# Mean products one row further back, and one weight half behind the last convolution

## The reference

```
x = layernorm(alpha * x + mixer(x))
x = layernorm(alpha * x + convffn(x))
```

```
gate, rnn = split(x @ w_in_c)
xc = causal_conv4(rnn)
r, i = sigmoid(xc . w_gate_a + b), sigmoid(xc . w_gate_x + b)   # 8 blocks of 128
log_a = 8 * r * log_sigmoid(lambda);  a = exp(log_a)
h = scan(a, sqrt(1 - a^2) * i * xc)
m = (gelu(gate) * h) @ w_out_c
```

## Time and profile before

| | |
|---|---|
| median of 3 runs | 1429.51 us |
| profiled execution | 1428.99 us |
| its span | 1426.9 us |
| TensorE busy | 1404.5 us (98%) |
| VectorE busy | 836.3 us (59%) |
| ScalarE busy | 620.4 us (43%) |
| GpSimd busy | 96.7 us (7%) |
| granted TensorE clock, mean | 0.997 |

### The profile page before, as it was taken

How to read it: one execution, slowest core, us unless ns; L and a number is a source line. 1 busy time by engine, 2 the same in 40 slices (tenths; PEclk the granted TensorE clock), 3 DMA queues, 4 the chain that set the end, 5 groups by cost and what they waited for, 6 DMA issues and landing times.

```text
span 1426.9 us, 24580 instructions
## 1 busy us (share of the span) xinstructions
PE 1404.5 (98%) x10244; PEld 1379.0 (97%) x10244; DVE 836.3 (59%) x1274; ACT 620.4 (43%) x1018; POOL 96.7 (7%) x112
## 2 busy tenths in 40 slices
PE   7999999999999999999999999999999999999996
PEld 7999999999999999999999999999999999999996
DVE  6656665656855644534455778888645455344555
ACT  5443535444654143412343577646632334124334
POOL 0010100000400000000000310024100000000002
PEclk9999999999999999999999999999999999999998
DMA  8131222234222322222222211222223222222222
GB/s 282 51 122 60 80 87 76 92 101 151 72 89 62 102 74 90 74 89 74 80 84 79 83 62 60 89 60 89 74 75 96 83 85 79 89 74 90 83 81 82
DMA packets 37231, 125.18 MB, mean 88 GB/s; under 512 B 4352, under 2 KB 6528, under 8 KB 36864
## 3 DMA queue, kind: packets, MB, share of 16 engines
q1 hardware_dynamic: 34128, 113.78, 25.1%
q0 software_dynamic: 2560, 8.91, 2.2%
q10 hardware_dynamic: 432, 0.91, 0.2%
HBM read 115.96 MB, written 7.63 MB: 87 GB/s over the span
## 4 chain that ended last, share of the span: by engine, by line
PE 92%; DVE 5%; ACT 1%; DMA 1%; issue 1%; SPq 0%; DVEq 0%; ACTq 0%
PE PS L637 28%; PE PS L638 28%; PE PS L639 28%; PE PS L909 1%; PE PS L806 1%; PE PS L815 1%; DMA raw<-weights 1%; DVE Y L1607 1%; PE PS L821 1%; DVE Y L1595 1%; PE PS L786 1%; PE PS L765 1%; PE PS L795 0%; PE PS L799 0%; PE PS L735 0%
## 5 line engine op out<-in xcount | busy, mean ns | idle before, releaser
L637 PE MATMUL PS<-xhi,whi 128*128 128x296 f32 (+1 forms) x2176 | 659.2, 303 | 7.7 <-DVE wlo L1323 7.5
L638 PE MATMUL PS<-xlo,whi 128*128 128x296 f32 (+1 forms) x2176 | 649.5, 298 | 0.0
L639 PE MATMUL PS<-xhi,wlo 128*128 128x296 f32 (+1 forms) x2176 | 647.8, 298 | 0.0
L637 PEld LDWEIGHTS PS<-xhi,whi 128*128 128x128 f32 x2176 | 411.3, 189 | 11.0 <-issue 8.0
L638 PEld LDWEIGHTS PS<-xlo,whi 128*128 128x128 f32 x2176 | 411.4, 189 | 1.4
L639 PEld LDWEIGHTS PS<-xhi,wlo 128*128 128x128 f32 x2176 | 410.2, 188 | 0.0
L637 PE MATMUL PS<-hhi,whi 128*128 128x296 f32 (+2 forms) x864 | 258.1, 299 | 0.4 <-DVE Y L1535 0.4
L1316 DVE TENSOR_TENSOR wlo<-raw,whi 128x1024 fp32r<-128x1024 f32 (+1 forms) x192 | 233.1, 1217 | 42.7 <-ACT whi L943 38.1
L943 ACT ACTIVATE whi<-raw 128x1024 fp32r<-128x1024 f32 (+1 forms) x192 | 199.7, 1043 | 131.5 <-PE PS L639 65.5
L638 PE MATMUL PS<-hlo,whi 128*128 128x296 f32 (+2 forms) x864 | 256.8, 297 | 0.0
L639 PE MATMUL PS<-hhi,wlo 128*128 128x296 f32 (+2 forms) x864 | 256.3, 297 | 0.0
(11 more groups left out here) (236 smaller groups left out, 1311.1 us busy)
## 6 DMA issues: line engine op xcount, KB each, us to landing
raw<-weights SPq DMA_DIRECT2D x182, 512.0 KB, 3.5
raw<-weights SPq DMA_DIRECT2D x16, 384.0 KB, 3.0
Y<-xT SPq DMA_DIRECT2D x8, 296.0 KB, 4.5
yT<-Y SPq DMA_DIRECT2D x16, 144.0 KB, 1.8
C<-consts SPq DMA_DIRECT2D x1, 2146.5 KB, 10.3
S<-s_hgrn POOLq DMA_DIRECT2D x4, 512.0 KB, 4.6
S<-s_ret POOLq DMA_DIRECT2D x4, 512.0 KB, 6.3
hgrn_out<-S POOLq DMA_DIRECT2D x4, 512.0 KB, 5.2
```

What stands on the lines that cost most here:

```text
L637: pe.matmul(dst, wh, h, start=first, stop=False)
L638: pe.matmul(dst, wh, lo, start=False, stop=False)
L639: return pe.matmul(dst, wl, h, start=False, stop=last)
```

## The change

Two edits. In `first_tiles` the two mean products of the second half are issued after steps 3 and 4 instead of steps 2 and 3, in the three stages `ln` 0 to 2. In VectorE's list of the recurrent block, round 12 makes its weight half (unit 122) after `convolve(7)` instead of ahead of `recurrence(2)`.

```diff
 CONV_AT = {0: 0, 1: 1, 2: 2, 4: 3, 7: 4, 8: 5, 11: 6, 12: 7}
+CONV_FIRST = (12,)
...
-                        if half == 0 and step == 2:
+                        if half == 0 and step == 3:
                             moments_of_second_half(ln, False)
-                        elif half == 0 and step == 3:
+                        elif half == 0 and step == 4:
                             moments_of_second_half(ln, True)
...
             for i in range(len(MIXER)):
                 if i in ROOT_AT:
                     one_minus_a2(ROOT_AT[i])
-                for v in weights_at(U_RNN + i):
-                    weights_lo(v)
+                if i not in CONV_FIRST:
+                    for v in weights_at(U_RNN + i):
+                        weights_lo(v)
                 if i in DECAY_AT:
                     log_a(DECAY_AT[i])
...
                 if i in CONV_AT:
                     convolve(CONV_AT[i])
+                if i in CONV_FIRST:
+                    for v in weights_at(U_RNN + i):
+                        weights_lo(v)
```

## The result

The changed kernel takes 1434.77 us, the median of six runs (1433.48 to 1435.33), against 1429.28 before (six runs): ratio 1.0037, interval 1.0027 to 1.0048. It is 5.5 us slower; forecast were +5.15 and 1434.6 us.

The account below looks back on a forecast made before the run. The prediction took TensorE's products (92% of the chain) plus its few waits as the bound. Mean products -0.75, stand +4.1 and clock fall +1.8 summed to +5.15 us, 1434.6 us, range 1431.3 to 1436.4.

Parts of the forecast that it names:

- The waits of line 863 go, 0.81 us a stage.: Three norm stages: mean products issued one step later no longer wait for VectorE's sums, 0.81 us a stage.
- Most is given back, 0.25 stays.: Norm stages: GpSimd's rows 3 and 5 hold TensorE, giving back 0.53 of 0.81; 0.25 a stage stays, -0.75 us in all.
- What it meets next is the norm's second half: Norm stages: TensorE, 0.81 us ahead, next meets second-half rows 3 and 5, whose cover is 0.74 and 0.45 us.
- The convolution gains 0.11 only.: Recurrent block, round 12: ScalarE's square root limits line 1805 to 912.97, so the convolution ends only 0.11 us earlier.
- The refill comes 10 us later and holds ScalarE.: Recurrent block: unit 124 issued at about 922.5 instead of 912.7; ScalarE's high half waits, the tanhs behind it 4.1 us later.
- The stand of 4.1 us.: Start of the output projection: TensorE stands, waiting for the late last GELUs; +4.1 us, ends +3.4 and +5.0.
- The clock falls, +1.8.: Behind the stand before the projection: TensorE's clock falls to the low level, +1.8 us, ends 0 and +3.4.
- The clock of the slice behind the stand: Sign in the new profile: granted clock at or below 0.9 in the slice behind TensorE's wait of about 4 us.
- The sum.: Whole kernel: -0.75 + 4.1 + 1.8 = +5.15 us, 1434.6 us; stall and fall given 0.62.
- The rival in which the clock stays up: Output projection: stall without the clock falling, net +3.35, 1432.9 us; chance 0.20.
- the whole early gain: Norm stages keep 2.4 us, rows 3 and 5 in time; with the stall 1431.2 to 1433.0 us; chance 0.08.
- the covered refill: Recurrent block: slack covers the late refill and nothing stands at the projection, 1428.6 us; chance 0.07.

Follow-up runs that it names:

- mean_short_low: Kernel before with only the mean products moved, and GpSimd's low halves cut to 32 columns (output partly wrong) in three stages: 1426.05 us, ratio 0.9978.
- mean_only: Kernel before with only the mean products moved to steps 3 and 4, weight half left ahead of the recurrence: 1429.04 us, ratio 0.9996.
- queue_order: Changed kernel, but in round 14 ScalarE makes unit 124's high half behind the gates' work, VectorE its low half at round's end: 1429.27 us, ratio 0.9998.
- fill_28: Changed kernel plus 28 spare products that nobody reads, keeping TensorE busy through the stand before the output projection: 1432.88 us, ratio 1.0020.
- half_only: Kernel before with only the weight half of unit 122 moved behind convolution 7: 1435.54 us, ratio 1.0039.
- fill_14: Changed kernel plus 14 spare products at the start of the stand, the rest of it quiet: 1434.04 us, ratio 1.0033.
- before_short_low: Kernel before, mean products at steps 2 and 3, with GpSimd's low halves cut to 32 columns in the three stages: 1428.43 us, ratio 0.9994.

## Why the prediction was right, step by step

- **The waits of line 863 go, 0.81 us a stage.** They go, and none is left, but 0.81 is under-sized. It counts the late starts alone; each mean product that waited also cost 0.10 behind its start. With the rows out of the way a stage gains 0.97 to 1.05 (mean_short_low), so the upper end of the term was about 3.1 us and not 2.4.
- **Most is given back, 0.25 stays.** The net is near (0.27, 0.2, 0.19 after; 0.61 in all in mean_only, for 0.75 forecast), and in part by luck: in the first stage 1.01 gained and 0.78 given back, for 0.81 and 0.53. Two errors of about 0.2 cancel. The step that failed is "What it meets next is the norm's second half". TensorE also meets rows 3 and 7 of the first half, and GpSimd's run of that half was never set against TensorE's steps (the earlier trace rows hold the second half alone). Row 3 of the second half does not hold it: the two earlier holds have cut TensorE's lead to about 0.5 us, less than that row's cover of 0.74. A hold also costs 0.11 behind its wait and not 0.07, and the weight load waits with it (the PEld line above), so nothing of it is done during the wait.
- **The convolution gains 0.11 only.** Right: VectorE's line behind the square root starts at 912.92 for 912.97 forecast, with 1.12 us of idle VectorE ahead of it. Of the 0.16 by which it comes earlier, 0.09 is the square root's own (911.63 for 911.72), so the edit itself gives 0.07.
- **The refill comes 10 us later and holds ScalarE.** Right in each link: issue 922.45 (forecast 922.5), landed after 3.5 us (3.4), high half at 926.01 (925.97). queue_order shows that it is the order of ScalarE's queue that turns this into TensorE's 4.1 us.
- **The stand of 4.1 us.** Right: 4.08 us waited, 940.35.
- **The clock falls, +1.8.** Right in kind and under-sized: 5.9 us of products ran at the low level in the profiled execution and cost 2.55, against the 3.8 us taken from the start. By medians, fill_28 puts it at about 2. The clock of the slice behind the stand was to show it at 0.9 or below; its mean is 0.90, which the page still prints as a 9, and only the finer stretches show the 0.50. How long it stays low varies from run to run, as the mean clocks say: those of the six executions lie between 0.994 and 0.997, those of half_only's five too, while all eleven of fill_28 have 0.997. The times follow these only roughly (1434.42 us at 0.997, 1433.48 at 0.996). Their spread of 1.9 us proves nothing by itself, since mean_only's eleven executions spread 2.0 at 0.997 and 0.998.
- **The sum.** 5.15 forecast, 5.5 measured. The mis-sizes are -0.75 for about -0.6, and 1.8 for 2 to 2.5. (1429.51 + 5.15 is 1434.7 and not 1434.6, which changes nothing.)
- The rival in which the clock stays up is refuted by the granted clock of 0.50, the whole early gain by the nine holds (its price would have been about 3.1 and not 2.4), and the covered refill by ScalarE's 5.2 us.

## What to carry to other kernels

Work moved behind a critical step also moves all that its completion sets free: here a 1.2 us operation, taken out of a gap that was idle anyway, held back a buffer's refill by 10 us. Look up who waits in order for that refill, and what stands behind it in the same queue; the late item itself may be needed by nobody yet. And where several engines feed one step by step, set each one's delivery against the new order over the whole stretch, the part before the moved operation included.

## What the runs showed of the hardware

In these executions the fall of the clock didn't follow the length of the quiet alone. After the kernel's last product it came 1.8 us later; in the changed kernel it came within 939.60 to 940.30, some 3.4 us into a stand; in fill_14, after 2.2 us of quiet, it came when TensorE had been at full pace again for a microsecond. A wait of 0.85 us (queue_order) left the clock at 1.00. The Trainium skill ("TensorE: Matmul & The Clock Gate", section "HAM oscillation — how this bites in real kernels") has the pattern that waits for DMA between groups of products throw TensorE back to half clock. The granted 0.50 after the stand, a wait for ScalarE, agrees, and fill_14 adds that a wait can be paid for after it has ended.

A short wait of TensorE cost more than its length: 0.10 us more behind a mean product (0.38 for 0.28 to the next product), 0.11 more behind a hold (0.24 to 0.25 for 0.135). A VectorE sum of 128x296 took 0.69 us beside GpSimd's whole rows and 0.47 beside its short ones (380.36 before, 380.37 in before_short_low).
